# A transformer stack on one core: rows by halves, norms' small steps reordered, weights split ahead of a change of block

## What is computed

```python
for i in range(2):                                  # stages "b1" and "f1", two layers
    h = rms_norm(x, attn_norm[i])
    proj = h @ w_in[i]                              # q, k, v of three attentions, three gates
    ...                                             # three attentions ya, yb, yc
    merged = g0 * (ya @ w_pa) + g1 * (yb @ w_pb) + g2 * (yc @ w_pc)
    x = x + merged @ w_out[i]
    h = rms_norm(x, mlp_norm[i])
    u = causal_depthwise_conv(h @ w_up[i], conv_w[i], conv_b[i])
    gate_u, val_u = jnp.split(u, 2, axis=-1)
    x = x + (jax.nn.silu(gate_u) * val_u) @ w_down[i]
```

## Time and profile before

| | us |
|---|---|
| median of 3 runs | 2651.52 |
| lowest and highest | 2649.44, 2652.42 |
| the profiled execution | 2651.22 |
| its span, first to last instruction | 2649.4 |
| PE busy in the span | 2567.8 |
| DVE, ACT, POOL busy | 1791.6, 1263.8, 116.4 |
| mean granted clock of PE | 0.988 |

### The profile page before, as it was taken

The page is one execution under the profiler, slowest core; times in us unless marked ns, Lnnn a source line. Parts: engine busy times, 40 slices in busy tenths (PEclk is TensorE's granted clock), DMA queues, the critical chain, the costliest instruction groups (busy, mean ns, idle before and its releaser), DMA issues.

```text
span 2649.4 us, 41203 instructions
## 1 busy us (share of the span) xinstructions
PE 2567.8 (97%) x16398; PEld 2177.5 (82%) x16398; DVE 1791.6 (68%) x2210; ACT 1263.8 (48%) x1485; POOL 116.4 (4%) x125
## 2 busy tenths in 40 slices
PE   6999999999999999999999999999999999999997
PEld 6886998878799988778998887678888888888886
DVE  5754776755577655345545643478988988988988
ACT  4451544553444431213334212067677677776775
POOL 1200000200000001200000111000000000000000
PEclk9999999999999999999999999989999999999999
DMA  6333553423555431136543311388998998999995
GB/s 236 122 144 119 193 188 143 144 98 128 189 191 185 142 136 65 65 127 215 190 175 129 127 68 61 116 324 350 352 359 338 348 358 342 344 361 339 353 356 207
DMA packets 77037, 558.19 MB, mean 211 GB/s; under 512 B 8672, under 2 KB 8800, under 8 KB 9568
## 3 DMA queue, kind: packets, MB, share of 16 engines
q1 hardware_dynamic: 76032, 550.93, 55.8%
q0 software_dynamic: 864, 5.24, 0.5%
HBM read 555.09 MB, written 1.05 MB: 210 GB/s over the span
## 4 chain that ended last, share of the span: by engine, by line
PE 89%; DVE 5%; ACT 3%; issue 2%; DMA 1%; DVEq 0%; SPq 0%; ACTq 0%; POOL 0%; POOLq 0%
PE bank L623 23%; PE bank L1104 17%; PE bank L1129 10%; PE bank L613 9%; PE bank L648 7%; PE bank L678 4%; PE bank L697 4%; PE bank L634 2%; PE bank L1077 1%; DVE w_lo L2294 1%; PE bank L1114 1%; PE bank L923 1%; PE bank L937 1%; PE bank L934 1%; ACT w_hi L1551 1%
## 5 line engine op out<-in xcount | busy, mean ns | idle before, releaser
L2294 DVE TENSOR_TENSOR w_lo<-ring,w_hi 128x2048 fp32r<-128x2048 f32 x216 | 486.3, 2288 | 54.0 <-ACT w_hi L1551 53.4
L1551 ACT ACTIVATE w_hi<-ring 128x2048 fp32r<-128x2048 f32 x216 | 405.0, 1916 | 20.5 <-PE bank L1104 16.8
L1104 PE MATMUL bank<-w_hi,xe_hi 128*128 128x512 f32 x792 | 311.2, 393 | 1.1
L1626 DVE TENSOR_TENSOR w_lo<-ring,w_hi 128x2048 fp32r<-128x2048 f32 x99 | 226.8, 2291 | 123.3 <-ACT w_hi L1213 121.2
L1104 PE MATMUL bank<-w_lo,xe_hi 128*128 128x512 f32 x792 | 308.7, 390 | 0.0
L1104 PE MATMUL bank<-w_hi,xe_lo 128*128 128x512 f32 x792 | 308.2, 389 | 0.0
L1213 ACT ACTIVATE w_hi<-ring 128x2048 fp32r<-128x2048 f32 x99 | 189.4, 1913 | 208.7 <-DMA ring<-in_stream 106.5
L623 PE MATMUL bank<-x_hi,w_hi 128*128 128x256 f32 x1008 | 285.3, 283 | 0.0
L623 PE MATMUL bank<-x_hi,w_lo 128*128 128x256 f32 x1008 | 285.2, 283 | 0.0
L623 PE MATMUL bank<-x_lo,w_hi 128*128 128x256 f32 x1008 | 285.2, 283 | 0.0
L613 PE MATMUL bank<-xT,ring 128*128 128x256 f32 x1088 | 254.7, 386 | 1.1 <-ACT Z L1470 1.1
(11 more groups left out here) (360 smaller groups left out, 4984.0 us busy)
## 6 DMA issues: line engine op xcount, KB each, us to landing
ring<-in_stream SPq DMA_DIRECT2D x431, 1024.0 KB, 4.9
yT<-in_stream SPq DMA_DIRECT2D x54, 1024.0 KB, 6.3
xT<-in_stream SPq DMA_DIRECT2D x27, 1024.0 KB, 6.5
Z<-in_stream SPq DMA_DIRECT2D x8, 1024.0 KB, 7.9
norm_rows<-in_rows POOLq DMA_DIRECT2D x4, 1024.0 KB, 6.5
cst<-in_cst SPq DMA_DIRECT2D x1, 1889.0 KB, 19.2
par<-in_par SPq DMA_DIRECT2D x1, 1502.0 KB, 15.2
xres<-in_x SPq DMA_DIRECT2D x2, 512.0 KB, 5.9
```

The lines of the kernel that those rows point to most:

```text
L1104: r = mm(banks[4 + j % 2], a[:, k, :], moe_part(b, i)[:, q * 512:(q + 1) * 512], start=(k == 0 and a is xe_hi and b is w_hi), stop=(k == K ...
L1551: act_(moe_part(w_hi, at), moe_slot(at), ACT.Copy).then_inc(*A.done("moe_hi", at))
L1626: v.tensor_tensor(part(w_lo, n), slot(f0 + n), part(w_hi, n).bitcast(F32), ALU.subtract)\
L2294: v.tensor_tensor(moe_part(w_lo, at), moe_slot(at), moe_part(w_hi, at).bitcast(F32), ALU.subtract)\
```

## The change

- **Banks one by one.** `project_out` and the last `rows_split` finish bank after bank (token block, then half) instead of both halves of a block together, and signal each; residual, sum of squares and LayerNorm's additions wait for their half. Of the out units, n = 2 is used until the last bank.
- **RMS norm.** The sum of squares is two instructions of 512 columns; the mean is two steps on DVE, the first (`rms_mean_begun`) after the first half. On ACT the last half's sum stands between the first two and the other six high pieces of block 0.
- **Order of turn and product.** `first_unit` runs `ahead` of the eight k of block 0's product (6; 4 in the mixer's layer 0; 8 in the dense FFN; 0 in the first layer), then turns block 1, pair by pair as block 0's low parts are read, then does the rest of block 0 and block 1.
- **Attention, layer 1.** Unit 1's high part is made before the norm, its low part in quarters (`between`) among the norm's steps.
- **Attention, layer 0.** Both token blocks are normalised first, then block 0's parts, then unit 0 is split in quarters, then block 1's parts, then unit 1. `first_unit` waits for quarters.
- **Lambda** of the differential attention moves from the block's start to the `vb` step (sums), the first score (exponential) and the first normalisation (difference).
- **LayerNorm.** "ln1": `centre(1)` ahead of `variance(1)`, and all of block 0's low parts ahead of `scale(1)`. "ln2": `variance(1)`, `centre(1)` ahead of block 0's low parts, six of which go ahead of `scale(1)`; on ACT both sums precede the high parts.

```diff
-            def first_unit(src, tag, l, ready, cleared, u, w, x):
-                for tb in range(TB):
-                    turn_block(src, tag, l, tb, ready[tb])
-                    if tb == 0:
-                        pe.wait_ge(*V.of("lo", u))
-                        if cleared:
-                            pe.wait_ge(*cleared)
-                    r = tokens_split(banks[3], w, x, (tb,), ready=lambda k: V.of("x_lo", tag, l, tb, k))
-                r.then_inc(*T.done("unit", u))
+            def first_unit(src, tag, l, ready, cleared, u, w, x, ahead, weights=None):
+                def product(tb, ks):
+                    return tokens_split(banks[3], w, x, (tb,), ready=lambda k: V.of("x_lo", tag, l, tb, k), ks=ks,
+                                        weights=None if tb else weights)
+                turn_block(src, tag, l, 0, ready[0])
+                if ahead:
+                    pe.wait_ge(*V.of("lo", u))
+                    if cleared:
+                        pe.wait_ge(*cleared)
+                    product(0, range(ahead))
+                turn_block(src, tag, l, 1, ready[1], lambda k: V.of("x_lo", tag, l, 0, k | 1))
+                if not ahead and not weights:
+                    pe.wait_ge(*V.of("lo", u))
+                product(0, range(ahead, KT))
+                product(1, range(KT)).then_inc(*T.done("unit", u))
...
-                steps += [(n, c, tb) for tb in range(TB) for n in (2, 3) for c in range(2)]
+                steps += [(n, c, tb, half) for tb in range(TB) for half in range(2) for n in (2, 3) for c in range(2)]
...
+                if last:
+                    order = [(c, tb, half) for tb in range(TB) for half in range(2) for c in range(2)]
...
                 if l:
                     sc.wait_ge(*T.of("unit", u0 - SPLIT))
                     split(0)
-                for tb in range(TB):
-                    rms_sum("b1", l, tb, V.of("x_out", "f1", l - 1, tb) if l else (s_x[tb], 16))
-                if l == 0:
-                    split(0)
+                    sc.wait_ge(*T.of("unit", u0 - 2))
+                    split(1)
+                    for tb, half in ((0, 0), (0, 1), (1, 0)):
+                        rms_sum("b1", l, tb, half, V.of("x_out", "f1", l - 1, tb, half))
+                    x_hi_out("b1", l, 0, f"attn_norm{l}", x1_hi, range(2))
...
+                    for tb in range(TB):
+                        for half in range(2):
+                            rms_sum("b1", l, tb, half, (s_x[tb], 16))
                     sc.wait_ge(s_head, 32)
+                    x_hi_out("b1", l, 0, f"attn_norm{l}", x1_hi)
+                    sc.wait_ge(*loaded(u0))
+                    for q in range(4):
+                        at = slice(q * 512, (q + 1) * 512)
+                        act_(first_hi[:, at], slot(u0)[:, at], ACT.Copy).then_inc(*A.done("hi", u0, q))
+                    x_hi_out("b1", l, 1, f"attn_norm{l}", x1_hi)
+                    split(1)
...
+            def rms_norm(tag, l, source, gain, hi, lo, between):
+                residual(*source, 0, 0)
+                residual(*source, 0, 1)
+                rms_mean_begun(tag, l, 0)
+                between(0)
                 rms_mean(tag, l, 0)
                 if tag == "f1":
                     rms_apply(tag, l, 0)
-                if source:
-                    residual(*source, 1)
+                residual(*source, 1, 0)
                 if tag == "b1":
                     rms_apply(tag, l, 0)
...
+                residual(*source, 1, 1)
+                rms_mean_begun(tag, l, 1)
+                x_lo_out(tag, l, 0, gain, hi, lo, range(2))
+                rms_mean(tag, l, 1)
+                x_lo_out(tag, l, 0, gain, hi, lo, range(2, 6))
                 rms_apply(tag, l, 1)
...
+                x_lo_out(tag, l, 0, gain, hi, lo, range(6, KT))
+                between(1)
                 x_lo_out(tag, l, 1, gain, hi, lo)
+                between(2)
+                between(3)
...
+                if tag == "ln2":
+                    variance(1)
+                    centre(1)
+                    if lo:
+                        lo(0, range(6))
+                else:
+                    if lo:
+                        lo(0, range(4))
+                    centre(1)
+                    variance(1)
+                    if lo:
+                        lo(0, range(4, KT))
                 scale(1)
```

More of the change, by code:

```diff
@@ L625, in features_split, with tokens_split @@
                 return r
-            def tokens_split(bank, w, x, blocks=(0, 1), ready=None):
+            def tokens_split(bank, w, x, blocks=(0, 1), ready=None, ks=range(KT), weights=None):
+                r = None
                 for tb in blocks:
-                    for k in range(KT):
+                    for k in ks:
+                        if weights:
+                            pe.wait_ge(*weights(k))
                         if ready:
@@ L695, in project_out @@
                     wv = slot(u).rearrange("p (c n) -> p c n", c=2)
-                    for half in range(2):
-                        r = mm(banks[2 * tb + half], gk[:, at + 2 * n + c, tb * P:(tb + 1) * P],
-                               wv[:, c, half * 512:(half + 1) * 512], start=(n == 0 and c == 0), stop=(n == 3 and c == 1))
-                    if (n, c, tb) == (3, 1, 0):
-                        r.then_inc(*T.done("rows", blk, l, 0))
-                    elif (c, tb) == (1, 1):
+                    r = mm(banks[2 * tb + half], gk[:, at + 2 * n + c, tb * P:(tb + 1) * P],
+                           wv[:, c, half * 512:(half + 1) * 512], start=(n == 0 and c == 0), stop=(n == 3 and c == 1))
+                    if (c, tb, half) == (1, 1, 1):
                         r.then_inc(*T.done("unit", u))
-                T.same(("rows", blk, l, 1), ("unit", u))
+                    elif (n, c) == (3, 1):
+                        r.then_inc(*T.done("rows", blk, l, tb, half))
+                T.same(("rows", blk, l, 1, 1), ("unit", u))
             def block1(l):
@@ L804, in block1 @@
                         T.same(("gate", l, 0), ("first", "f1", l))
-                T.same(("rows", "f1", l, 1), ("unit", u))
+                T.same(("rows", "f1", l, 1, 1), ("unit", u))
             def rotate(l, i):
@@ L834, in swiglu @@
                         T.same(("dense_gate", 0), ("first", "f2", 0))
-                T.same(("rows", "f2", 0, 1), ("unit", u))
+                T.same(("rows", "f2", 0, 1, 1), ("unit", u))
             def rwkv(l, fill, conformer):
@@ new lines, in block1 @@
+                if l:
+                    split(0)
+                    rms_norm("b1", l, ("f1", l - 1), f"attn_norm{l}", x1_hi, x1_lo,
+                             lambda q: quarter(1, q, in_half(1), A.of("hi", u0 + 1)))
+                else:
+                    rms_mean_begun("b1", l, 0)
+                    rms_mean("b1", l, 0)
+                    rms_apply("b1", l, 0)
+                    rms_mean_begun("b1", l, 1)
+                    rms_mean("b1", l, 1)
+                    rms_apply("b1", l, 1)
+                    x_lo_out("b1", l, 0, f"attn_norm{l}", x1_hi, x1_lo)
+                    for q in range(4):
+                        quarter(0, q, first_hi, A.of("hi", u0, q))
+                    x_lo_out("b1", l, 1, f"attn_norm{l}", x1_hi, x1_lo)
+                    split(1)
@@ L1741, in qk_norm, with neg_lambda @@
+                def neg_lambda():
+                    ve.wait_ge(*A.of("lamexp", l))
+                    v.scalar_tensor_tensor(out=sm("neglam", 1), in0=sm("lamexp", 2)[:, 1:2], scalar=-lam_init,
+                                           in1=sm("lamexp", 2)[:, 0:1], op0=ALU.add, op1=ALU.subtract)\
+                        .then_inc(*V.done("neglam", l))
                 def qk_norm(i):
@@ L1823, in block1 @@
                     ffn_split(u0 + N_IN1 + N_PROJ + N_OUT, n)
[L1824 removed]
+                rms_norm("f1", l, ("b1", l), f"mlp_norm{l}", x_hi, x_lo, lambda i: None)
                 def evacuate(kind, j):
@@ L1928, in mixer @@
                     for tb in range(TB):
-                        residual("f1", DEPTH - 1, tb)
+                        for half in range(2):
+                            residual("f1", DEPTH - 1, tb, half)
                     for tb in range(TB):
```

171 lines of the change are left out of this document (89 added, 82 removed).

## The result

The changed kernel takes 2620.36 us (median of 4 executions, 2618.95 to 2621.42) against 2651.97 on the same chip: ratio 0.9882, 95% interval 0.9865 to 0.9899. It is 1.2% faster. The forecast was 2626.2, so 5.8 us of gain were not foreseen, and the time lies just outside the range (2621.0 to 2638.5). The profiled execution took 2621.42.

A forecast was written before the change was run, and what follows sets the result against it. PE is 89% of the chain and 97% busy, so only its waits and half-speed work could be won. Terms 8.0 + 5.0 + 3.9 + 3.8 + 1.7 + 1.3 + 1.3 = 25.0 us; 2651.2 - 25.0 = 2626.2; range 2621 to 2638.5.

The forecast's parts named there:

- FFN to attention: Change into layer 1: earlier turn and unit 1's weight cut in advance gain 5.0 us, bounds 3.4 and 5.5.
- LN1: Mixer to dense FFN, layer 0: centre(1) and scale(1) leave block 0's path; gain 3.9 us, bounds 2.3 and 4.4.
- first mixer: FFN to mixer, layer 0: one residual fewer ahead of block 0's low pieces, held-back k's; gain 1.7 us, bounds 1.0 and 1.9.
- The zero for untouched code: Stretches outside the changes, such as both attentions: forecast gain 0, the sum simply taken from the profiled 2651.2.
- The clock at the second LayerNorm: Dense FFN to mixer: PE still idles 2.5 us and falls to the lower level; gain 3.8 us, bounds 2.0 and 4.4.
- rival (b): Clock still falls at two more changes and the start runs at half speed: 2632 us; chance 0.08.
- The start: Layer 0: norm first, unit 1 starts near 23.7 instead of 31.99; gain 8.0 us, bounds 5.5 and 8.6.
- Attention to FFN: Two places: earlier turn of block 1 and filled wait against later half sums; gains 0.8 and 0.5 us, together -0.4 to 2.0.
- Mixer to experts: Experts' entry: centre(1) leaves the path between variance and scale; gain 1.3 us, bounds 0.8 and 1.9.
- rival (d): Slower: clock stays low after changed boundaries, placed at the experts' entry; 2676 us at twice the deciding matmul count; chance 0.03.
- (a): The norms' halves bring nothing; only start, weight cut ahead and moved centre gain, about 13 us, 2638; chance 0.08.
- (c): At the start DMA decides: unit 1 or 2 waits for the ring, 8 becomes 2, 2632 us; chance 0.05.

The follow-up runs named there:

- halves_undone: Changed kernel with rows ended block by block and RMS sums of squares whole over 1024 columns, LayerNorm adds still in halves; 2623.23 us, ratio 0.9898.
- start_alone: Kernel before with only layer 0's start changed (norm first, unit 0 split in quarters, turns ahead of products), lambda's place as before; 2646.44 us, ratio 0.9985.
- before_gap_filled_2: Kernel before with seven unread matmuls of 128 columns inside the 2.08 us gap of each attention layer; 2649.30 us, ratio 0.9994.
- start_undone: Changed kernel with only layer 0's start back in the old order; 2632.64 us, ratio 0.9934.
- turn_order_undone_2: Changed kernel with only PE's old order at the changes of block (all eight k, block 1's turn, block 1's product), second run; 2628.48 us, ratio 0.9913.
- gap_moved: Changed kernel with five unread matmuls behind the transposes of layer 0's first block, ahead of unit 2; 2623.76 us, ratio 0.9908.
- lambda_back: Changed kernel with only lambda's sums, exponential and small products back in their old place, with the two waits; 2625.74 us, ratio 0.9910.
- combined: Changed kernel with the late transfers and unread matmuls in gaps of attention, second LayerNorm, router and last scatter; 2611.62 us, ratio 0.9858.
- dma_order_2: Second run, with more rounds, of the changed kernel with norm and group rows and remaining parameters and constants transferred later; 2617.52 us, ratio 0.9880.
- dma_order: Changed kernel with norm and group rows asked for after unit 2, remaining parameters and constants behind unit 2's weight; 2619.70 us, ratio 0.9889.

## Why the forecast was 5.8 us short

By the traces the gain is 29.8 us against 25.0. The other 1.0 of the 5.8 is between single executions: the changed kernel's profiled one was its slowest (2621.42, median 2620.36).

**Boundaries: three near, their mechanisms right in part.** FFN to attention 5.0 against 5.15, LN1 3.9 against 4.1, first mixer 1.7 against 1.4. The runs confirm the weight ahead (3.8), the held-back k's (1.0, and 0.8 to 0.9 at the mixer) and the LayerNorms' order. They do not confirm the half residual, 0.55 at the mixer and 0.65 at LN1: halves_undone loses nothing at either. And a part is clock in both kernels: start_alone wins 0.81 and 1.30 at two of them unchanged.

**The zero for untouched code: wrong, the largest part.** The step is "The forecast is 2651.2 - 25.0", with no term outside the changes: the profiled execution of before was taken as it was there. But it had half-speed matmuls in both attentions and in the second mixer (1505.7 to 1509.1), and the changed one has none there: 1.4 + 1.5 + 0.9 = 3.8 us. The runs put the attention's part down to the fall itself (before_gap_filled_2). For the mixer it is inferred from traces: start_undone and turn_order_undone_2 have that fall and win 1.32 and 1.43 where the changed kernel wins 2.25. No gap of 2 us stands ahead of it. In the kernel before PE ran 16 matmuls of two columns, idled 0.34 us, and fell in the small matmuls after it:

```profile
1502.37 1.84 PE L876 MATMUL bank<-cst,Z 128*128 128x2 f32 x16
1504.55 1.82 PE L898 MATMUL bank<-Z 64*64 64x128 f32 x48 [0.34 <-DVE small L2077]
1505.00:1510.00 5.00, 5.00 (x94) 4.39 (x87) 4.04 (x8) 0.00 (x0) 1.05 (x2) 0.66 0.34 141
```

**The clock at the second LayerNorm: mis-sized.** The step was "PE still idles 2.5 us and falls to the lower level as it does now". PE idles 2.44 us (3.05 in the kernel before) and did not fall in two traces of three: measured 5.4 and 5.5 where I had 3.8. Where it does fall the stretch wins 4.84 (changed kernel), 3.92 (start_undone) or 3.46 (gap_moved), so 3.8 was fair for its premise, and whether the premise holds changes from one execution to the next: luck, not reading. The prediction counted on falls that vanish at two changed boundaries, but had no term for such falls elsewhere; its rival (b) let the clock only cost.

**The start: 8.0 is near, by luck in part.** "Lands 8.1 us later" was read from one execution; the same load took 10.2 in the second trace of before, and 10.4, 8.9 and 8.7 in the changed kernel's. Unit 1 came at 25.73, 24.34 and 24.24 and not at 23.7, unit 2 at 32.21 in the first trace and not at 30.1. The comparison was made with an early start of before, by 1.8 us. The sum there was also only reachable because lambda moved: "cost 0.2 us at most" was the wrong price for moving a wait past a split, as lambda_back shows (4 to 5.5). In the sum itself, 10.2 and 1.3 make 11.5 and not 11.6, which changes nothing.

**Attention to FFN: 1.0 and 1.2 to 1.4 against 0.8 and 0.5.** turn_order_undone_2 loses 1.0 and 0.8 to 1.0 here, so the held-back k's bring as much as the whole gain in layer 0; I had let the later half sums eat more.

**Mixer to experts.** 1.3 of forecast against 2.25, of which 0.9 is the mixer's fall. The 20 us of low clock there stayed, and rival (d) did not come.

**Rivals.** (a) is refuted as a whole (2638 against 2620) but holds at the first mixer and the LayerNorms. (c) is refuted in size by start_undone (7.1 to 8.6 us and not 2), while its mechanism is there: with the rows asked for later the start is 4 us shorter. (b) named the right quantity with the wrong sign.

**Open.** What in the timing of a gap decides whether the clock falls was not isolated: gap_moved was to move one gap with all else equal, and moved it too little. That the fall costs what attention gained is shown; that the changed kernel will keep its gaps free of it is not.

## What to carry to other kernels

Count half-speed matmuls in the trace before costing an edit: here those behind gaps of 2.1 to 2.5 us, and those in the mixers' small matmuls, came and went when something ahead of them had moved, also in code that the edit leaves alone, so give them a term with both signs. When a piece of work is moved, price the waits that stand in front of it together with what queues behind them; two sums of 0.3 us held up 4 us here. Take the same instruction in several traces and compare stretch by stretch; it resolved a few tenths of a us here where whole times scatter by 2, as long as the low clock in each trace was listed beside it.

## What the runs showed of the hardware

- A gap of 2.08 us on PE was followed by low clock in 11 of 32 attentions; each cost 1.4 to 2.2 us. Seven unread matmuls of 128 columns (1.83 us) inside it took it away. A gap of 2.44 us at the second LayerNorm was followed by it in 8 of 13 traces.
- The clock also fell where PE hardly idled: in the mixers, behind 16 matmuls of two columns and 0.34 us of idle time (all four falls of before's two traces there), and in combined, where no gap from 1686.8 to 1703 was longer than 0.7 us and low clock stood at 1691.2 to 1694.6, behind the router's 32 matmuls of 8 columns, and at 1698.0 to 1701.4 in the gather.
- 1.5 MB of rows asked for by POOL at 1.3 us, and used after 1180 us: with them x's second half landed 8.1 to 10.5 us after its issue (16 traces), without them 4.7, 5.1 and 6.0 (dma_order_2, dma_order, combined).
